# Where and from what a 16 MB zero fill is written in a two-block transformer kernel

## The reference, cut to what matters

```
def reference(...):
    x = first_block(x, ...)          # layer 0: mla_mixer, layer 1: dilated_mixer, each with swiglu
    return second_block(x, ...)

# second_block, in each layer
y_a = diff_post(diff_attention_latent(qa, ka, va, ka_c, va_c, lam), ...)
y_b = spatial_gating(...)
y_c = neighbourhood_attention(...)
h = h + gt1 * merge_branches(p[..., OFF_GATE:], y_a, y_b, y_c, w_branch[l], w_out[l])
...
y = hier_moe(xn2, moe_w_group, ..., moe_w_down)      # 2 of 32 experts per token
h = h + gt2 * y
```

## Time and profile before

| | us |
|---|---|
| median of three runs | 3377.62 |
| the three runs | 3375.18 to 3380.16 |
| the profiled execution, as timed | 3387.09 |
| its span in the trace | 3385.4 |
| TensorE busy in the span | 2808.1 (83%) |
| VectorE, ScalarE, GpSimd busy | 1278.2, 871.1, 1088.5 |
| moved by DMA | 780.65 MB, 231 GB/s over the span |

### The profile page before, as it was taken

How to read it: one execution, slowest core, us unless ns; L and a number is a source line. 1 busy time by engine, 2 the same in 40 slices (tenths; PEclk the granted TensorE clock), 3 DMA queues, 4 the chain that set the end, 5 groups by cost and what they waited for, 6 DMA issues and landing times.

```text
span 3385.4 us, 35632 instructions
## 1 busy us (share of the span) xinstructions
PE 2808.1 (83%) x13137; PEld 1839.0 (54%) x13137; DVE 1278.2 (38%) x2368; ACT 871.1 (26%) x1198; POOL 1088.5 (32%) x507
## 2 busy tenths in 40 slices
PE   4889879999899898689984988887697885988885
PEld 2668757767777666467862423332575773333331
DVE  2632134444323422863344322222426443322223
ACT  0243312224333311432221211112324331111111
POOL 0068656652676243033421000000353660000000
PEclk8989989999899999899987999998798997999998
DMA  8545568871454453022245999999342467999997
GB/s 305 170 130 185 177 227 287 291 280 53 148 173 151 149 162 121 17 85 82 95 149 205 391 399 398 399 395 373 108 125 68 157 223 279 394 399 399 399 400 277
DMA packets 218653, 780.65 MB, mean 231 GB/s; under 512 B 15076, under 2 KB 16274, under 8 KB 168608
## 3 DMA queue, kind: packets, MB, share of 16 engines
q1 hardware_dynamic: 189856, 669.61, 53.7%
q0 software_dynamic: 28672, 109.36, 9.4%
HBM read 733.58 MB, written 62.62 MB: 235 GB/s over the span
## 4 chain that ended last, share of the span: by engine, by line
PE 51%; DMA 22%; DVE 13%; SPq 6%; POOL 4%; ACT 2%; issue 2%; DVEq 0%; POOLq 0%; ACTq 0%
PE banks L731 11%; PE banks L732 10%; PE banks L736 10%; DMA arena<-in_moe_w_gate 4%; DMA weight_ring<-in_moe_w_down 4%; PE banks L1125 4%; SPq L600 4%; POOL weight_ring_r L1720 3%; DMA weight_ring<-in_moe_w_up 3%; DMA x_transposed<-in_moe_w_up 3%; PE banks L1148 2%; DMA weights_high<-in_moe_w_gate 2%; PE banks L864 2%; DMA rel_rows<-arena 1%; SPq L608 1%
## 5 line engine op out<-in xcount | busy, mean ns | idle before, releaser
L1720 POOL TENSOR_TENSOR weight_ring_r<-weight_ring,weights_high_r 128x2048 fp32r<-128x2048 f32 x136 | 620.7, 4572 | 519.8 <-ACT weights_high_r L1376 429.3
L1376 ACT ACTIVATE weights_high_r<-weight_ring 128x2048 fp32r<-128x2048 f32 x136 | 257.4, 1901 | 741.2 <-PE banks L736 327.3
L731 PE MATMUL banks<-weights_high_r,x_transposed_r 128*128 128x512 f32 x1008 | 403.8, 401 | 36.0 <-ACT weights_high_r L1376 12.2
L1857 POOL DMA_DIRECT2D moe_y<-arena x64 | 33.9, 530 | 935.5 <-DVE arena L2537 919.6
L736 PE MATMUL banks<-weight_ring_r,x_transposed_r 128*128 128x512 f32 x1328 | 325.2, 391 | 2.2 <-POOL weight_ring_r L1720 2.0
L1720 POOL TENSOR_TENSOR weight_ring_r<-weight_ring,gates_r 128x2048 fp32r<-128x2048 f32 (+1 forms) x60 | 270.8, 4522 | 136.3 <-ACT gates_r L1376 74.7
L736 PEld LDWEIGHTS banks<-weight_ring_r,x_transposed_r 128*128 128x128 f32 x1328 | 249.4, 188 | 57.4 <-POOL weight_ring_r L1720 5.6
L731 PEld LDWEIGHTS banks<-weights_high_r,x_transposed_r 128*128 128x128 f32 x1008 | 194.0, 192 | 91.4 <-issue 25.6
L1582 ACT ACTIVATE arena<-banks 64x1024 f32<-64x1024 f32 x64 | 65.3, 1021 | 610.3 <-PE banks L1125 610.3
L732 PE MATMUL banks<-weights_high_r,arena_r 128*128 128x512 f32 x520 | 207.2, 398 | 0.0
L2519 DVE TENSOR_TENSOR arena<-banks,arena 64x1024 f32<-64x1024 f32 x64 | 77.9, 1217 | 315.6 <-ACT arena L1582 315.6
(11 more groups left out here) (378 smaller groups left out, 4884.1 us busy)
## 6 DMA issues: line engine op xcount, KB each, us to landing
weight_ring<-in_moe_w_down SPq DMA_DIRECT2D x62, 1024.0 KB, 30.7
weight_ring<-in_w_in SPq DMA_DIRECT2D x56, 1024.0 KB, 5.2
weight_ring<-in_w_ada SPq DMA_DIRECT2D x48, 1024.0 KB, 7.3
weight_ring<-in_ffn_w_in SPq DMA_DIRECT2D x44, 1024.0 KB, 5.1
weight_ring<-in_dil_w_qkv SPq DMA_DIRECT2D x36, 1024.0 KB, 5.1
tokens_out<-in_moe_w_gate SPq DMA_DIRECT2D x34, 1024.0 KB, 29.8
arena<-in_moe_w_up SPq DMA_DIRECT2D x34, 1024.0 KB, 28.9
weight_ring<-in_moe_w_up SPq DMA_DIRECT2D x34, 1024.0 KB, 29.0
```

Source lines behind the costliest of these rows:

```text
L731: nc.tensor.matmul(banks[t][:, 0:width], xh, wh[:, k, :], start=k0 + k == 0, stop=False)
L1376: nc.scalar.activation(high(s, kn, width), slot(c, kn, width), ACT.Copy).then_inc(high_ready, 1)
L1720: nc.gpsimd.tensor_tensor(slot(c, kn, width, ring_r), slot(c, kn, width), high(s, kn, width), ALU.subtract).then_inc(low_ready, 1)
```

## The change

The fill is split in two. At the beginning POOL writes only one block of zeros, 128 rows of 4 KB (512 KB), to a new HBM tensor `zeros`. The two big transfers now stand in layer 0 of the second stack, behind the request of `da_subln_g` and ahead of the load of bias 4, and read this block over and over: they go from HBM to HBM, with the same pieces of 4 KB and the same destinations. ScalarE waits for the small transfer alone. POOL's wait ahead of the scatter stays.

```
+        zeros_dram = nc.dram_tensor("zeros", [P, D], F32, kind="Internal").ap()
+        zeros_made = sem("zeros_made")
...
-            act.wait_ge(zero_out, 32)
+            act.wait_ge(zeros_made, 16)
             attention(mla_units())
...
-            nc.gpsimd.dma_start(xs_dram.rearrange("(r p) d -> p r d", p=P),
-                                Y[:, 2048:2048 + D].unsqueeze(1).broadcast_to([P, xs_dram.shape[0] // P, D])
-                                ).then_inc(zero_out, 16)
-            nc.gpsimd.dma_start(ys_dram[NE * CAP:, :].rearrange("(r p) d -> p r d", p=P),
-                                Y[:, 2048:2048 + D].unsqueeze(1).broadcast_to([P, MAX_OVER * CAP // P, D])
-                                ).then_inc(zero_out, 16)
+            nc.gpsimd.dma_start(zeros_dram, Y[:, 2048:2048 + D]).then_inc(zeros_made, 16)
             pool.wait_ge(misc_ask, seen.next(misc_ask))
...
                 row(I["da_subln_g_2"][layer], P)
+                if layer == 0:
+                    pool.wait_ge(zeros_made, 16)
+                    nc.gpsimd.dma_start(xs_dram.rearrange("(r p) d -> p r d", p=P),
+                                        zeros_dram.unsqueeze(1).broadcast_to([P, xs_dram.shape[0] // P, D])
+                                        ).then_inc(zero_out, 16)
+                    nc.gpsimd.dma_start(ys_dram[NE * CAP:, :].rearrange("(r p) d -> p r d", p=P),
+                                        zeros_dram.unsqueeze(1).broadcast_to([P, MAX_OVER * CAP // P, D])
+                                        ).then_inc(zero_out, 16)
                 base = na_before(layer)
                 for k in range(4, len(biased)):
```

## The result

| | us |
|---|---|
| before, median of seven runs | 3375.18 (3369.07 to 3380.16) |
| changed, median of seven runs | 3356.58 (3346.13 to 3366.53) |
| ratio, with its 95% interval | 0.9949 (0.9931 to 0.9966) |
| changed, the profiled execution's span | 3361.2 |

The changed kernel is faster by 18.6 us, 0.5%. The forecast was 3357.6, with 3353 to 3366 as its range.

The account below looks back on a forecast made before the run. VectorE, waiting for rel_rows behind the zeros in GpSimd's queue, was taken to bound the beginning. Gains of 19.9 and 0.1 us, with the copy costing 0, off the 3377.62 us median gave 3357.6, range 3353 to 3366.

Parts of the forecast that it names:

- What bounded the beginning: VectorE waits 38.9 us at line 2207 for rel_rows, queued behind 16 MB of zeros; without them it lands at 27.9 us.
- The gain of 19.9 us: At the beginning, VectorE's second normalisation starts at 53.14 us instead of 73.03.
- Nothing else late there: At the beginning, mla_w_uq loads land in time even at 11.5 us each; ScalarE's and GpSimd's waits cost nothing.
- TensorE's clock: At the transposes and product after the shortened gap, a higher clock gives 0.1 us, between 0 and 1.9.
- The copy's duration: At the neighbourhood attention, the zeros copied from HBM to HBM take 55 us, between 41 and 91.
- The nearest row: Profile row of an HBM-to-HBM copy in 1.5 KB pieces, 316 GB/s from 142 to 170 us; basis for 55 us.
- The spare time: At the neighbourhood attention, zeros may end 68.4 us after issue before bias 5 is late; 13 us to spare, cost 0.
- The sum: Whole kernel: 19.9 plus 0.1 us off the median of 3377.62 gives 3357.6 us.
- The rivals: Slow copy with late biases, chance 0.05; half-slow copy, 3367.6 us, 0.08; something else holding the beginning, 0.03.
- Late biases: At the neighbourhood attention, a 91.2 us copy delays the biases by 22.8 us, giving 3380.5 us; chance 0.05.
- something else holds the beginning: At the beginning, rel_rows still lands late, costing only if over 25 us; no effect would give 3377.6; chance 0.03.
- that sign: Sign of being wrong: the shift of 20 us at 85 us is smaller at 1360 us.

Follow-up runs that it names:

- The order alone: Kernel before with the two zero transfers issued behind the three rel_rows transfers instead of ahead, still from SBUF at the beginning; ratio 0.9948, median 3357.39 us.
- the second: The changed kernel run once more, word for word, against the kernel before; ratio 0.9928 (0.9905 to 0.9951), median 3351.4 us.

## Why the prediction was right, point by point

**What bounded the beginning: right.** The order alone gives the whole gain, with the DMA engines as full as ever. The landing of `rel_rows` was forecast at 27.9 us; it lands between 24 and 25 (issued up to 21.45, landing in 3.1).

**The gain of 19.9 us: right, and a little small.** The second normalisation starts at 52.62, forecast 53.14; the product ahead of it ended 0.5 us earlier in this execution (52.15 for 52.63). Against the profile of before it is 20.4 us, and 20.6 at the issue of `rel_rows_repeated`. Over all profiles that issue is at 139.0 to 139.9 us in the three with the wait and at 115.9 to 119.8 in the seven without it, on average 21.5 us earlier: the pair that the first comparison shows is one of the smaller gains.

**Nothing else late there: right.** `mla_w_uq` landed in 4.4 us, and in the run with the order swapped in 11.6 without holding TensorE up, which is the case that the prediction had worked out with the old landing times.

**TensorE's clock: half right.** The six transposes take 1.00 us instead of 1.54, and the four 1.11 as before; so the level fell between them, as forecast. From the second normalisation to the product it is 8.01 us instead of 8.42, a gain of 0.4. But the product that follows took longer, 25.55 us against 24.02. From 60 to 67 us the granted clock is 0.53, the lower level:

```profile
60.00:67.00 7.00, 6.38 (x9) 2.72 (x9) 1.23 (x3) 0.00 (x0) 0.00 (x0) 0.53 0.00 0
```

In the profile of before it began at 81.45, and only the first 3 us were at the lower level, as the same view of that kernel says (0.56 is 4.4 us of 5 at the lower level):

```profile
80.00:85.00 5.00, 4.38 (x9) 1.99 (x8) 0.89 (x3) 0.00 (x0) 0.00 (x0) 0.56 0.01 3
```

The prediction allowed the clock a gain between 0 and 1.9 us and no loss; in this pair it was 0.4 us of gain and 1.5 of loss. The loss cannot be laid to the change: over the profiles the product takes 24.02, 24.19 and 25.22 us with the wait ahead, and 24.04 to 25.55 without it. It opens at the lower level in either case, for some 3 us in one profile and some 6 in another.

**The copy's duration: right.** 56.8 us from first issue to last landing, forecast 55 between 41 and 91. The nearest row was the right one to take: its 316 GB/s came back as 311 to 316. By that row's rate the prediction's own working gave 53 + 6 = 59 us, and it took 55, since the pieces are larger and the engines free. The rate was the same 316; it was start and end that came to some 4 us instead of 6. The Trainium skill's page "DMA: Bandwidth & Descriptors", section "Latency and other measured facts", gives 214 GB/s per direction for copies of tiles with rows of 16 KiB between HBM tensors, issued from the sync and scalar queues, and 207 where the rows of neighbouring partitions lie 512 KiB apart. The prediction read this as an upper limit for its own copy and took the 512 KiB as its own case. They are not: the copy is issued by GpSimd, its 128 rows lie 4 KiB apart, and 512 KiB lie between the successive pieces of one of them. The measured 311 to 316 GB/s are half as much again, and they decide.

**The spare time: right in kind, 1 us off in size.** Bias 5 was named as the tight one, and it is the one that VectorE waits for with 4 MB more. The limit was put at 68.4 us after the first issue. In the changed kernel 56.8 us left 10.6 us to spare, which puts it at 67.4. From the zeros' end to the end of bias 4's mask it was 3.9 us, not 2.4, and from there to bias 5 5.75 and not 5.5; in return VectorE wanted bias 5 0.6 us later.

**The sum: right, and its closeness in part luck.** 20.0 us off the median of before. Measured 18.6 us in the first comparison and 26.4 in the second (3377.84 less 3351.4); the intervals of the two ratios overlap, from 0.9931 to 0.9951, which is 17 to 23 us. The first median is 1.0 us from the forecast; the second, of the same kernel, is 6.2 us away and below the forecast's range.

**The rivals.** Late biases did not occur, and the two kernels with more to copy show that they would have cost about what was said, a microsecond for each beyond the limit. With 4 MB more the last copy ends 70.9 us after the first issue, 3.5 beyond 67.4, and the stretch grows by 2.7; with 16 MB more it ends 110.8 us after it, 43.4 beyond, and the stretch grows by 41.3. What the prediction left out of this price is TensorE's clock after a long wait, which made 5 us between the two kernels with 16 MB more. That something else holds the beginning is ruled out by `rel_rows`, which lands at 24.6 us.

**What was not foreseen:** the wait that went had also evened out the engines' variation ahead of it. The prediction expected every step from the scatter to the end to be shifted by the same 20 us, and named a smaller shift at 1360 us as a sign of being wrong. In the first pair of profiles that sign appeared: 20.6 us at the first attention, 17.5 at the `da_subln_g` request. But the second profile of the changed kernel is 33.6 us ahead there, and that of the kernel with the order alone 27.7, so the sign was not usable: single profiles of one kernel drift apart by 16 us at this place.

## What to carry to other kernels

A small transfer that an engine waits for should not stand behind a large one in the same queue. Look at its landing time and at that of a similar one ahead of the large transfer; here 49.0 against 4.9 us named the cause, and putting the small one first was enough, without moving a byte elsewhere.

A large transfer has a price that depends on what is issued behind it in its queue and when that is wanted. It was nothing at one place and the whole gain 74 us later in the program, at the same rate and with the same engines. To place one, write down for each later transfer of that queue when its data are wanted, and compare the tightest with the large one's end.

## What the runs showed of the hardware

- Transfers of GpSimd's queue land in order behind a 16 MB one (49 us for 24 KB, 35.5 us for 2 MB), while SP's loads beside the same transfer only get slower (4.4 to 11.6 us for 768 KB at the beginning).
- A copy from HBM to HBM runs at 311 to 316 GB/s, with the DMA share at 0.97 to 0.99, where the same zeros out of SBUF together with weight loads reach 407. It makes no difference whether 512 KB are read 32 times or 16 MB once (53.2 and 53.0 us).
- Such a copy did not slow the attention beside it (102.0 us with it, 101.3 to 103.8 without it).
- After a wait of 39 us TensorE resumed at a granted clock of 0.50, and for how long it stayed there differed: of two kernels whose work behind the wait is the same, one took 5 us longer over it. After a wait of 20.5 us, 32 matmuls took 10.37 us instead of 7.42.
